# A delta-net mixer's input projection in pairs of weight blocks by seven products, on one Trainium2 core

## The reference

```python
def gdn_mixer(h, w_in, conv_w, a_log, dt_bias, norm_g, w_out):
    proj = h @ w_in                       # 1024 x 4112: q, k, v, z of 8 heads, and 16 columns b, a
    qkv, z, b_logit, a_logit = jnp.split(proj, [p1, p2, p3], axis=-1)
    qkv = jax.nn.silu(causal_dwconv(qkv, conv_w))      # 4 taps along the tokens
    ...
    o = rms_norm(o, norm_g) * jax.nn.silu(z...)        # z gates the output of the recurrence
    return o.reshape(B, T, GDN_VAL).astype(h.dtype) @ w_out
```

## Time and profile before

| | |
|---|---|
| median of three runs | 3073.09 us |
| the profiled execution | 3074.86 us |
| its span, first to last instruction | 3073.1 us |
| TensorE matmul, busy | 3000.0 us, 98% |
| VectorE, busy | 2056.7 us, 67% |
| ScalarE, busy | 1382.9 us, 45% |
| GpSimd, busy | 731.9 us, 24% |
| mean granted TensorE clock | 0.991 of full speed |

### The profile page before, as it was taken

One profiled execution on the slowest core, in us unless ns is written; L12 is line 12 of the kernel. 1 busy time (PEld: TensorE's weight loads), 2 busy tenths in 40 slices (PEclk: granted clock), 3 DMA queues, 4 the chain that ended last, 5 costly groups with the idle time before them and its releaser, 6 DMA issues.

```text
span 3073.1 us, 44859 instructions
## 1 busy us (share of the span) xinstructions
PE 3000.0 (98%) x17070; PEld 2453.1 (80%) x17070; DVE 2056.7 (67%) x2833; ACT 1382.9 (45%) x2556; POOL 731.9 (24%) x706
## 2 busy tenths in 40 slices
PE   8999999999999999999999999999999999999997
PEld 7788888887788788877888788878888778878876
DVE  7275647547888777777555566643854788877777
ACT  4435545346777421134111366644533677751212
POOL 0019300000666533320000022100000056653332
PEclk9999999999999999999999999999999999999999
DMA  3110331003666976522222221213100366697653
GB/s 135 35 49 22 112 121 42 28 35 148 228 243 245 342 267 246 205 96 96 96 95 96 80 76 55 58 50 123 49 28 29 136 237 243 246 333 283 246 203 125
DMA packets 167575, 428.90 MB, mean 140 GB/s; under 512 B 12128, under 2 KB 45168, under 8 KB 165616
## 3 DMA queue, kind: packets, MB, share of 16 engines
q1 hardware_dynamic: 128576, 386.79, 34.5%
q10 hardware_dynamic: 38832, 39.85, 3.8%
HBM read 286.08 MB, written 140.51 MB: 139 GB/s over the span
## 4 chain that ended last, share of the span: by engine, by line
PE 78%; DVE 10%; ACT 4%; issue 3%; DMA 2%; POOL 2%; SPq 0%; ACTq 0%; DVEq 0%; POOLq 0%
PE ps L2960 18%; PE ps L2976 14%; PE ps L3182 10%; PE ps L3183 10%; PE ps L3184 10%; PE ps L3409 2%; DMA hid_store<-staged 2%; PE ps L3339 2%; PE ps L3032 1%; DVE work L1892 1%; DVE work L1908 1%; DVE hres L1923 1%; PE ps L3541 1%; PE ps L3414 1%; PE ps L3299 1%
## 5 line engine op out<-in xcount | busy, mean ns | idle before, releaser
L2960 PE MATMUL ps<-act,whi 128*128 128x512 f32 x2384 | 751.5, 396 | 5.4 <-DVE work L2043 2.7
L2960 PEld LDWEIGHTS ps<-act,whi 128*128 128x128 f32 x2384 | 444.1, 188 | 114.6 <-issue 13.9
L2960 PE MATMUL ps<-act,wlo 128*128 128x512 f32 x1192 | 466.8, 392 | 0.0
L1876 DVE TENSOR_TENSOR wlo<-wraw,whi 128x1024 fp32r<-128x1024 f32 x255 | 319.1, 1253 | 208.7 <-ACT whi L986 175.1
L2976 PE MATMUL ps<-act,whi 128*128 128x512 f32 x1376 | 369.8, 390 | 0.7 <-DVE work L2450 0.7
L2335 DVE TENSOR_TENSOR work<-work,ps 128x512 f32<-128x512 f32 x360 | 241.0, 684 | 141.9 <-PE ps L3184 140.0
L883 POOL TENSOR_TENSOR stagedf<-quads 128x1024 f32<-128x1024 f32 x28 | 74.8, 2670 | 1067.4 <-ACTq L1277 1053.1
L2976 PEld LDWEIGHTS ps<-act,whi 128*128 128x128 f32 x1376 | 258.0, 188 | 56.7 <-issue 1.8
L1336 ACT ACTIVATE whi<-wraw 128x1024 fp32r<-128x1024 f32 x112 | 116.6, 1057 | 414.3 <-POOL wraw L902 350.5
L986 ACT ACTIVATE whi<-wraw 128x1024 fp32r<-128x1024 f32 x148 | 155.8, 1057 | 310.5 <-DMA wraw<-wstream_dram 306.9
L2960 PEld LDWEIGHTS ps<-act,wlo 128*128 128x128 f32 x1192 | 223.8, 188 | 49.4
(11 more groups left out here) (384 smaller groups left out, 6342.8 us busy)
## 6 DMA issues: line engine op xcount, KB each, us to landing
wraw<-wstream_dram SPq DMA_DIRECT2D x260, 512.0 KB, 3.5
hid_store<-staged SPq DMA_DIRECT2D x196, 512.0 KB, 3.5
act<-hid_store SPq DMA_DIRECT2D x42, 1024.0 KB, 11.3
hresr<-hid_store SPq DMA_DIRECT2D x56, 512.0 KB, 11.7
qkvz<-work ACTq DMA_DIRECT2D x32, 512.0 KB, 2.6
work<-qkvz ACTq DMA_DIRECT2D x64, 256.0 KB, 3.2
tx<-hid_store SPq DMA_DIRECT2D x28, 512.0 KB, 7.9
act<-hid_store SPq DMA_DIRECT2D x28, 512.0 KB, 12.1
```

The costliest lines, as they stand in the source:

```text
L1876: TT(wlo[s][:], wraw[s][:], whi[s][:].bitcast(F32), ALU.subtract).then_inc(w_split, 1)
L2960: last = mm(out_of(u)[:, 0:width], (wlo if hl else whi)[s][:, at:at + P], rhs(kt, xp, e), start=kt == hl == xp == 0, stop=kt == kts - 1 an ...
```

## The change

Of the 29 full blocks four stay as they are: b and a, and q, k, v of one head. 24 blocks become 12 pairs of two neighbouring blocks, q with k and v with z of six heads, each by the seven products. The last z stays a full block. So that this comes out, the heads are taken in the order 0, 7, 1, 2, ..., 6, and z of head 7 is the last block.

- The plan: pair p uses slots 0 and 1 (p even) or 2 and 3 (p odd), and banks 0 to 2 or 4 to 6.
- The input's sums T1 to T4 are made once, while the four full blocks run. ScalarE scales the residual in `hres` by the norm's gain in place (16 operations), VectorE subtracts quarters (`sum_raw`, 8 operations of 128x1024), ScalarE rounds the sums into free work buffers (`sum_hi`, 8), VectorE leaves the low parts in `hres` (`sum_lo`, 8).
- As `hres` is overwritten, SP stores the residual to `hsave` before the stage (`save_residual`, three DMAs, 4 MB) and loads it back during the recurrence; VectorE waits for it (`h_back`) at the mixer's end.
- Each pair adds `weight_sums` on GpSimd, the sums' high parts on ScalarE, their low parts on VectorE, three copies out on ScalarE, three additions on VectorE; the norm's factor is applied at the end (`pair_scaled`). VectorE's `split_lo` of a pair's blocks waits until GpSimd has made all four sums, since it overwrites what they read.
- The order of VectorE, ScalarE and TensorE is written out without loops. `log_decays` stands in pair 2, the convolution and gate of a head in the pairs of the next.
- GpSimd clears the two buffers of the recurrence that VectorE cleared.
- At the exit TensorE does the first half of the last z block before the first transposes, and ScalarE waits until the seven gates have been stored.

```diff
+HEAD_ORDER = (0, 7, 1, 2, 3, 4, 5, 6)
+GPAIRS = 2 * (GDN_H - 2)
 ...
-            full("mix1b", [n % 4 for n in range(4, 33)])
+            full("mix1b", [n % 4 for n in range(4, 8)])
+            here("mix1p")
+            for p in range(GPAIRS):
+                blocks = [plan.block(2 * (p % 2) + k) for k in range(2)]
+                banks = {"1": 0, "6": 0, "7": 0, "4": 0, "5": 1, "3": 1, "2": 2}
+                for name in UP:
+                    u = plan.fixed((4 if p % 2 else 0) + banks[name])
+                    if name in "24":
+                        plan.after[blocks["24".index(name)]] = u
...
 SP:
+            def save_residual():
+                for first, e, new in ((slice(0, KT), 0, 8), (slice(0, 4), 1, 12), (slice(4, KT), 1, 16)):
+                    sp.wait_ge(h_new, 32 + new)
+                    sp.dma_start(hsave[:, first, E[e]], hres[:, first, E[e]]).then_inc(h_saved, 16)
...
                     if n == plan.at["out1"][0] + 3:
+                        sp.wait_ge(fpe[1].sem, fpe[1].at("o", 2))
+                        sp.wait_ge(unit_done, pair_unit(GPAIRS - 1, "4") + 1)
+                        sp.dma_start(hres[:], hsave).then_inc(h_back, 16)
                         sp.wait_ge(fpe[1].sem, fpe[1].at("o", NCH - 1))
+                    if layer and n == plan.at["mix1b"][0]:
+                        save_residual()
...
 GpSimd, after the first layer's MLP:
+            for p in range(GPAIRS):
+                weight_sums(pair_blocks(p), [wraw[plan.slot[n]][:, E[e]] for n in pair_blocks(p) for e in range(2)], up_sums[p % 2])
+            pool.wait_ge(unit_done, pair_unit(GPAIRS - 1, "4") + 1)
+            for t in (15, 13):
+                nc.gpsimd.memset(unit(t), 0.0).then_inc(gla_zero, 1)
...
 ScalarE:
+                for p in range(GPAIRS):
...
+                    kept(p, "1", (0, 0), used[0])
+                    if p and p % 2 == 0:
+                        gate(HEAD_ORDER[m - 1], c - 1, pair_unit(p - 1, "4") + 1)
+                    kept(p, "5", (1, 1), used[1])
+                    if p + 1 < GPAIRS:
+                        pair_hi(p + 1, 0)
+                    kept(p, "6", (0, 1), used[0])
+                    if p % 2:
+                        silu(c)
+                    if p + 1 < GPAIRS:
+                        pair_hi(p + 1, 1)
+                        sums_hi(p + 1)
+                    else:
+                        split_hi(plan.at["mix1z"][0])
+                    if p % 2:
+                        silu(c + 1)
+                    else:
+                        silu(c - 1)
...
 VectorE:
+                fresh(4)
+                fresh(5)
+                split_lo(n0)
+                fresh(6)
+                fresh(7)
+                split_lo(n0 + 1)
+                conv(0, u0)
+                conv(1)
+                split_lo(n0 + 2)
+                sum_raw(0)
+                sum_raw(1)
+                split_lo(n0 + 3)
                 scaled(u0, unit(7))
+                sum_raw(2)
+                sum_lo("T1")
+                sum_raw(3)
+                conv(2)
+                scaled(u0 + 1, unit(0))
+                conv(3, u0 + 2)
... (b and a copied out)
+                scaled(u0 + 2, unit(1))
+                eng.wait_ge(x_sum, 2 * PREPS + 2)
+                split_lo(pair_blocks(0)[0])
+                sum_lo("T2")
+                conv(4, u0 + 3)
+                eng.wait_ge(x_sum, 2 * PREPS + 2)
+                split_lo(pair_blocks(0)[1])
+                sums_lo(0, 0, 1)
+                sum_lo("T3")
+                scaled(u0 + 3, unit(10))
+                sum_lo("T4")
+                for p in range(GPAIRS):
+                    c = 3 * (p // 2 + 2)
+                    more = p + 1 < GPAIRS
+                    if p == 0:
+                        eng.wait_ge(evac, u0 + 4)
+                    if p % 2:
+                        conv(c, pair_unit(p - 1, "4") + 1)
+                        if more:
+                            eng.wait_ge(x_sum, 2 * (PREPS + p + 1) + 2)
+                        split_lo(pair_blocks(p + 1)[0] if more else plan.at["mix1z"][0])
+                        conv(c + 1)
+                    elif p:
+                        conv(c - 1, pair_unit(p - 1, "4") + 1)
+                    if p % 2 == 0:
+                        eng.wait_ge(x_sum, 2 * (PREPS + p + 1) + 2)
+                        split_lo(pair_blocks(p + 1)[0])
+                    if p == 2:
+                        log_decays()
+                    corner(p, "2", (0, 0))
+                    if more:
+                        eng.wait_ge(x_sum, 2 * (PREPS + p + 1) + 2)
+                        split_lo(pair_blocks(p + 1)[1])
+                    corner(p, "7", (1, 1))
+                    if more:
+                        sums_lo(p + 1, 0)
+                    corner(p, "3", (0, 1))
+                    if more:
+                        sums_lo(p + 1, 1)
+                    pair_scaled(p)
+                    if p == 0:
+                        conv(5)
...
+                conv(3 * GDN_H - 1, uz)
+                split_lo(plan.at["out1"][0])
...
 TensorE, for each pair and each of its products:
+                        if name in "152":
+                            eng.wait_ge(evac, plan.need[u] + 1)
+                        if name in "15":
+                            eng.wait_ge(w_split, pair_blocks(p)[int(name == "5")] + 1)
+                        if name in "67":
+                            eng.wait_ge(read_act, reads + (1 if name == "6" else 3))
+                            eng.wait_ge(x_split, 2 * x + (1 if name == "6" else 2))
+                        if name == "4":
+                            eng.wait_ge(read_dve, reads + 2)
...
+                last_gate((0, 1, 2, 3))
+                eng.wait_ge(evac, plan.at["mix1z"][1])
                 raw_keys(0, 0)
                 raw_queries(0, 0)
                 decays(0, 0)
-                last_gate((0, 1, 2, 3))
```

372 lines of the change are left out of this document (232 added, 140 removed).

## The result

The changed kernel takes 3085.62 us (median of 7, 3078.15 to 3087.91) where the kernel before took 3073.09 (median of 7) on the same chip: 12.5 us more, ratio 1.0033 with a 95% interval of 1.0023 to 1.0043. Slower, by about what had been forecast (3087). Its profiled execution took 3085.59, its span is 3083.6, 10.5 more than that of before.

A forecast was written before the change was run, and what follows sets the result against it. TensorE was taken as the bound, with VectorE its supplier. Gain -30.8, entry +9, pauses in the pairs +21, clock +8 and exit +6.5 gave +13.7: 3087 us against the median, forecast range 3077 to 3094, with rivals 3060 to 3100.

The forecast's parts named there:

- Gain 30.8: Twelve pairs: 144 fewer matmuls, a pair every 19.35 us, save 30.8 us if TensorE never waits.
- Odd pairs: Pairs 5, 7, 9: VectorE waits for GpSimd's sums, so product 4 comes late, 2.1 us each; pair 11 2.0.
- Entry 9: Start of the paired stage: VectorE's queue, held up by GpSimd's sums, makes TensorE late, costing 9 us.
- Pair 1 6.3: Pair 1: three convolutions, splits, corners and four GpSimd operations fill VectorE, pausing TensorE 6.3 us, partly at product 6.
- Pair 2 3.3: Pair 2: the 4.8 us of log_decays stand before the correction of product 2, pausing TensorE 3.3 us.
- Pair 3 3.3: Pair 3: VectorE starts late and is caught by all four sums, pausing TensorE 3.3 us.
- Clock 8: Behind TensorE's pauses near or above 2 us the clock drops to 1.2 GHz, costing 8 us in all.
- Exit 6.5: From the last pair to the recurrence: late gdn_first and ScalarE's wait for the gate's landing cost 6.5 us more.
- A: Rival: the sums slip into VectorE's idle time, x_sum before 9 us in an odd pair; 3055 us, chance 0.15.
- B: Rival: pauses exist but stay below 1.8 us, so the clock holds; 3066 to 3073 us, chance 0.2.
- C: Rival: every odd pair meets all four sums, at 11.5 us; 3098 us, chance 0.15.
- the prediction's 4.4: Where VectorE does busy SBUF work, a set of four GpSimd sums holds it up 4.4 us, 1.1 per operation.

The follow-up runs named there:

- cheap sums: Changed kernel, but from pair 2 on GpSimd zeroes three sum buffers and the fourth sum takes 64 columns (output wrong): 3065.63 us, ratio to before 0.9966.
- nine moves: Changed kernel with nine moves of order at the entry, in the pairs and at the exit, no other work: 3059.09 us, ratio to before 0.9948.

## Why the prediction was right, and where it was right by luck

The total was right, in part by luck; its parts, from the full blocks' start to the first inverse product, were expected at +13.7 and measured at +4.8 and +7.2 in the two profiles of the changed kernel.

- **Gain 30.8.** Confirmed: a pair that nothing holds up takes 19.37 (19.35 expected), and -30.7 is what the 12 would have given.
- **Odd pairs.** The mechanism and the size were right: the sums at 10.5 (10.3 expected), product 4 at 18.73 (18.7), pauses of 1.9 to 2.0 (2.1) in 5, 7, 9 and 11. Both things that make it were shown by taking each away.
- **Entry 9, measured 5.6 and 7.8.** Over-sized. The pause before the fourth full block was 2.10 and not 3.4, since the four operations beside GpSimd lost 3.8 together and not 4.4 (0.9 for a step of a convolution; the 1.1 of the earlier trace rows was another operation's), and VectorE's queue ahead of them was 0.6 shorter than counted. The second half, for which all four sums of pair 1 were set to hit VectorE, depends on when the sums start: 50.9 us after S, with four operations held up, or 52.4, with three.
- **Pair 1 6.3, measured 5.7**, in two pauses: 3.12 ahead of product 6, on `kept` behind `conv(5)` and `silu(5)`, and 2.03 ahead of product 4. **Pair 2 3.3**, measured 4.5, by the logarithms as said: a pause of 2.50, the rest with the lower clock behind it. Even pairs were counted against 16.3 where odd ones had 16.6 for the same place; with 16.6 its term is 3.0. **Pair 3 3.3, measured 2.0**: one step of its convolution was held up, not all that the four sums could reach.
- **Clock 8, measured about 5 in the stage.** The step that failed in kind: it priced a pause by its length. Three of ten pauses were followed by the lower clock, and the longest was not. The price of one stretch was right, though not by the nine starts where fourteen fit, which make 1.1 us: it is half of the 3.2 us at 0.50, and pair 5, with such a stretch, took 1.6 more than pairs 7 and 9.
- **Exit 6.5, measured 7.4.** Both named waits were there, `gdn_first` 8.3 us after z's start (8.6 expected) and `state_decay` at 17.4 (16.8); taking each away gave 3.0 and 2.0.
- **Not in the sum at all:** the recurrence, 287.0 and 287.3 from q to X against 282.4 to 284.9, with 31 us at 1.2 GHz instead of 10 to 17; and 3 us ahead of the stage, whose cause is open. Changed kernels with a short stretch there took 282.6 to 283.2, although they too load the 4 MB of `hres` back in it; so these loads, which the sum had at 0 to 2, do not make the recurrence's 4 us. With medians over the profiles (all eleven of changed kernels for S, the two of the changed kernel for the rest), 3.1 + 6.0 + 4.3 - 1.0 (from X to the end) = 12.4 of the 12.5 measured. So half of the loss came through terms that were over-sized, and half from where nothing was forecast.

Of the rivals, A was refuted at its own deciding point (the sums at 10.5, not before 9) and became true in the kernel with cheap sums. B's short pauses (one of 1.72 in pair 3, the others 1.94 to 2.04) and C's stretched ones were not seen.

The rule of the Trainium skill ("SBUF — State Buffer", section "Who interferes with whom") is borne out in the part that no row of before could show. In the single lines of the changed kernel (ns min/median/max), the first step of a convolution, a tensor_scalar, is held up beside GpSimd just as the two-input steps are:

```profile
L2058 DVE TENSOR_SCALAR work<-work,pvec x24: 740/752/1779, 1418.1 to 1722.6; 128x1024 f32<-128x1024 f32 x24
...
L2062 DVE SCALAR_TENSOR_TENSOR work<-work,pvec x84: 1281/1284/2383, 40.6 to 1726.9; 128x1023 f32<-128x1023 f32 x28, 128x1022 f32<-128x1022 f32 x28, 128x1021 f32<-128x1021 f32 x28
```

Beside GpSimd's sums this happened twice, at 1442.18 and 1492.37, for 1.0 us each. Both are among the four operations that the four sums of a pair held up there, so nothing came on top of the prediction's 4.4. A third tensor_scalar, at the exit, was held up beside GpSimd's two memsets, which did not hold up two-input steps above (VectorE, then GpSimd):

```profile
1722.62 1.62 DVE L2058 TENSOR_SCALAR work<-work,pvec 128x1024 f32<-128x1024 f32 x1
...
1721.85 1.85 POOL L1014 MEMSET work<- 128x1024 f32 x2 [30.13 <-PE ps L3617]
```

An operation with one input in PSUM lost nothing: `scaled` at 1473.43, inside GpSimd's sum of 1472.38 to 1474.64, took its usual 1.21 us.

## What to carry to other kernels

When matmuls are traded for work on the suppliers, their busy share (VectorE 17.55 of 21.6 us in an odd pair) does not say whether they keep up: follow one pair from its start and ask what stands in the queue between the latest input and the first operation that TensorE waits for. Here one convolution of 5 us put behind two short corrections turned a loss of 12 us into a gain of some 4 (ratio 0.9986, 0.9976 to 0.9995), and more such moves made it 19, with no work taken away. In a stage that one engine's queue bounds, a pause taken away alone comes back a few operations later; and look past the stage's end, since pauses there can slow what follows.

## What the runs showed of the hardware that had not been expected

- GpSimd's memset (0.53 us for 128x512) doesn't slow VectorE's two-input operations beside it, but a tensor_scalar beside two memsets took 1.62 us instead of 0.75. GpSimd's two-input sums take VectorE's two-input operations from 1.28 to 2.2 and from 1.22 to 2.3 us, and a tensor_scalar from 0.75 to 1.78, and are slowed themselves, from 1.3 to 2.27.
- The lower clock does not follow from a pause's length alone: 3.12 us of pause without it (window 1494.70 to 1498.70 at 1.00) and 2.03 with it, in one execution; and one and the same pause of 2.10 was followed by it in four profiles of seven. At the recurrence's start it lasted from 10 to 31 us in 14 profiles; at 27 to 31 us the recurrence took 286.1 to 287.3 from q to X, at 10 to 17 it took 282.4 to 284.9. Shorter pauses at the exit went mostly, not always, with the short stretches: the kernel with nine moves had 24 us of it. What decides was not settled.
- A first pair that began 1.6 us earlier, as the clock had stayed up, let GpSimd start its sums 1.5 us earlier and ended 2.2 us later; in the three such profiles it ended later than in all four of the others.
